# Values stationary in half-columns for two heads at once in three attentions, and a recurrence without filler products

## The chip, the cores and the metric

The kernel runs on one core of a Trainium2 chip. The metric is the device time of one execution in microseconds: median 3224.0 us of three runs (3223.61 to 3229.15).

## What is computed

Two transformer blocks of two layers each, at 512 latent tokens (and 256 context tokens in the second block), width 1024, in float32. Their large matrix products (projections, gated sums, MLPs of width 4096) take most of the time. The change touches three of the four attentions and one recurrence:

```python
# dsa: 8 heads of 64, one k and v for all heads, causal, keys chosen by an index score, ALiBi
# mla: 16 heads, q and k of 64 + 32 (rotary), v of 64, causal
# sw (gqa_attend / banded_window_attention): 8 heads of 64, 2 kv heads, a window of 3 blocks
#   of 128 keys and 256 context keys, with a sink logit in the softmax
probs = jax.nn.softmax(logits, axis=-1)
o = einsum(probs, v)
# mlstm_dir: a recurrence over chunks of 128 tokens, 4 heads of 128, in two directions
s = einsum(qc, kc) * exp(d_log - m_t)
num = inter_w * einsum(qc, c_mat) + einsum(s, vc)
h = num / max(abs(den), exp(-m_t))
c_new = carry_w * c_mat + einsum(w, kc, vc)
```

The attention of the last layer (cat, heads of 128) keeps its form.

## The kernel before

The program is written engine by engine; each engine has its own instruction list, and semaphores order them. The large products use split float32: an operand is x_hi (rounded, made by ScalarE) and x_lo (the rest, made by VectorE), and three products are summed (lines 785 to 787). Weights come by DMA into wbuf; ScalarE makes w_hi of one unit of a stage, VectorE w_lo (line 2011), and a unit of products waits for both. A stage's products are set off by `split_pair`, which takes the activations tile by tile (k) as x_lo is ready (line 2017).

The attentions dsa, mla and sw run through `attention_ahead` on TensorE and VectorE and through `attention` on ScalarE. A unit is one head of one block of 128 queries. mla and dsa go through the query blocks backwards, so key blocks per unit are 4, 3, 2, 1 (16 units each in mla, 8 each in dsa); sw has 8 units each of 4, 5, 5, 4, 2, 2. In one step of TensorE's list:

- `logits` (line 911) of unit u into psA;
- `turn_probs` of an earlier unit: its probabilities, one 128 x 128 transpose per key block (line 756), into psB. The lead is 2 units in dsa and mla, 1 in sw;
- `weigh_values` (line 928) of the unit before that: per key block one product with the transposed probabilities as the stationary 128 x 128 operand and v (128 x 64) as the streaming one, into psO, which holds two rows of ROW_H = 8 units.

VectorE masks the logits and takes their negated maximum (line 1990 in one instruction, in mla lines 1995 and 1997), ScalarE takes the exponential with its sum and copies the transposed probabilities out of psB. After a row of 8 units VectorE's `finish` takes the reciprocal of the sums (line 1976) and multiplies (line 1981) into a token-major tile. At the end of each attention TensorE turns these tiles feature-major (16 transposes in dsa, 32 in mla, 24 in sw), ScalarE copies them out, and only then are the operands of the output projection split. In mla ScalarE does that, and the first two w_hi, between the copies. dsa ends in `meet`, a barrier of all engines. In sw, TensorE first turns the recurrence's result hs, and VectorE multiplies it out (line 2584).

In the recurrence there are twelve steps (six chunks, two directions). In a step TensorE does `lstm_scores` of the step after next (first a filler product `keep_clock` of 512 columns, line 747, then four products with 4 rows, line 1225, and four scores, line 1228), `lstm_values` (lines 1249, 1250) and `lstm_keys` (line 1236). VectorE does the mask (line 2538), `lstm_finish` (lines 2516 to 2529), the state (line 2553) and two weighings (lines 2544, 2546). Four such filler calls stand ahead of or behind the stages as well.

The only place where products go to groups of columns of the array is `mod_rows` (line 1085): four products of 32 stationary columns and 384 streaming ones, each to its own 32 partitions of psO.

## Time and profile before

| what | value |
|---|---|
| median of three runs | 3224.0 us |
| the profiled execution, its own time | 3223.06 us |
| its span (first to last instruction) | 3221.2 us |
| PE busy | 3064.1 us (95%) |
| DVE busy | 1627.2 us (51%) |
| ACT busy | 1239.2 us (38%) |
| mean granted clock of TensorE | 0.972 of full speed |
| dsa, from the first logits to the first output product | 144.3 to 223.0 us |
| mla, the same | 843.4 to 949.2 us |
| recurrence, first product to last filler | 1712.7 to 1801.1 us |
| sw, first logits to first output product | 1801.1 to 1936.6 us |

The profile is one execution. PE is TensorE's products, PEld its weight loads, DVE VectorE, ACT ScalarE, POOL GpSimd. Products overlap, and their ends are modelled, so distances between starts say more than durations. PEclk is the granted clock as a share of 2.4 GHz; 0.50 is 1.2 GHz. "DVEq" or "issue" in a chain is an engine's own queue.

### The profile page before, as it was taken

The page shows a single profiled execution, that of the slowest core. Times are in us where ns is not written, and L with a number is a line of the kernel's source. Part 1 is how long each engine was busy: PE and PEld are TensorE (multiplying, and loading weights), DVE is VectorE, ACT ScalarE, POOL GpSimd, SP SyncE. Part 2 cuts the span into 40 slices and gives each one's busy share as a digit, 9 for nine tenths or more (in the row PEclk, how much of TensorE's full clock was granted, in tenths as well). Part 3 has the DMA queues.
Part 4 walks back from the last instruction along what each step waited for, and adds up shares of the span by engine and source line. Part 5 has one row for each costly group of instructions (what it writes and reads, how often), then busy time and mean ns, then how long its engine had stood idle before and what let it go on. Part 6 is the DMA issues. An engine that isn't in the chain of part 4 may idle for free.

```text
span 3221.2 us, 39495 instructions
## 1 busy us (share of the span) xinstructions
PE 3064.1 (95%) x15144; PEld 2473.4 (77%) x15144; DVE 1627.2 (51%) x2430; ACT 1239.2 (38%) x2054; POOL 155.2 (5%) x142
## 2 busy tenths in 40 slices
PE   7989999999999999999998988999999899899999
PEld 5667778867777778867886777888888776778887
DVE  4864677674454677675226443432333634344344
ACT  3444333335564333345123452432222444443333
POOL 2200000011000000010003002000000100000000
PEclk9979999999999999999998999999999999999999
DMA  5102443433202443421120001112121110022222
GB/s 195 53 19 74 163 176 137 162 108 59 73 18 75 163 176 138 161 86 53 53 79 1 1 1 53 53 54 76 52 78 52 52 55 24 1 84 99 104 84 73
DMA packets 159713, 259.22 MB, mean 80 GB/s; under 512 B 54316, under 2 KB 74154, under 8 KB 159468
## 3 DMA queue, kind: packets, MB, share of 16 engines
q1 hardware_dynamic: 157844, 252.66, 22.6%
q10 hardware_dynamic: 1628, 4.78, 0.4%
q8 instruction: 73, 1.20, 0.2%
q14 instruction: 40, 0.33, 0.0%
q0 software_dynamic: 128, 0.26, 0.0%
HBM read 255.59 MB, written 2.10 MB: 80 GB/s over the span
## 4 chain that ended last, share of the span: by engine, by line
PE 86%; DVE 6%; ACT 4%; issue 2%; DVEq 1%; ACTq 1%; POOLq 0%; DMA 0%; PEldq 0%; PEld 0%
PE psA L785 23%; PE psA L786 22%; PE psA L787 22%; PE psB L756 3%; PE psA L742 3%; PE psA L911 3%; ACT work L1316 2%; PE psO L928 2%; PE psO L873 1%; PE psA L991 1%; ACT w_hi L1316 1%; PE psA L801 1%; DVE work L2129 1%; PE psA L803 1%; PE psA L802 1%
## 5 line engine op out<-in xcount | busy, mean ns | idle before, releaser
L1316 ACT ACTIVATE w_hi<-wbuf 128x1024 fp32r<-128x1024 f32 (+1 forms) x349 | 368.2, 1057 | 1170.7 <-PE psA L787 1147.4
L785 PE MATMUL psA<-act_hi,w_hi 128*128 128x512 f32 (+1 forms) x1872 | 708.9, 379 | 44.0 <-DVE act_lo L2017 29.3
L2011 DVE TENSOR_TENSOR w_lo<-wbuf,w_hi 128x1024 fp32r<-128x1024 f32 (+1 forms) x349 | 429.3, 1233 | 567.6 <-ACT w_hi L1316 563.3
L786 PE MATMUL psA<-act_lo,w_hi 128*128 128x512 f32 (+1 forms) x1872 | 700.0, 374 | 0.0
L787 PE MATMUL psA<-act_hi,w_lo 128*128 128x512 f32 (+1 forms) x1872 | 698.6, 373 | 0.0
L785 PE MATMUL psA<-hid_hi,w_hi 128*128 128x512 f32 (+1 forms) x1280 | 477.5, 373 | 5.4 <-DVE work L2129 4.5
L786 PE MATMUL psA<-hid_lo,w_hi 128*128 128x512 f32 (+1 forms) x1280 | 472.1, 369 | 0.0
L787 PE MATMUL psA<-hid_hi,w_lo 128*128 128x512 f32 (+1 forms) x1280 | 471.5, 368 | 0.0
L785 PEld LDWEIGHTS psA<-act_hi,w_hi 128*128 128x128 f32 x1872 | 357.4, 191 | 115.0 <-issue 33.2
L786 PEld LDWEIGHTS psA<-act_lo,w_hi 128*128 128x128 f32 x1872 | 357.6, 191 | 62.6 <-issue 2.6
L787 PEld LDWEIGHTS psA<-act_hi,w_lo 128*128 128x128 f32 x1872 | 357.0, 191 | 62.2
L2129 DVE TENSOR_TENSOR work<-work,psA 128x512 f32<-128x512 f32 (+1 forms) x256 | 192.7, 753 | 262.2 <-PE psA L787 254.4
L785 PEld LDWEIGHTS psA<-hid_hi,w_hi 128*128 128x128 f32 x1280 | 241.2, 188 | 68.5 <-issue 19.9
L787 PEld LDWEIGHTS psA<-hid_hi,w_lo 128*128 128x128 f32 x1280 | 241.1, 188 | 41.4
L786 PEld LDWEIGHTS psA<-hid_lo,w_hi 128*128 128x128 f32 x1280 | 241.4, 189 | 38.3
L2151 DVE SCALAR_TENSOR_TENSOR work<-work,small 128x768 f32<-128x768 f32 x224 | 221.6, 1030 | 1.5
L1316 ACT ACTIVATE work<-psA 128x512 f32<-128x512 f32 (+2 forms) x239 | 150.5, 633 | 162.2 <-PE psA L787 145.3
L1316 ACT ACTIVATE work<-psA,small 128x128 f32<-128x128 f32 (+6 forms) x232 | 128.6, 573 | 206.4 <-DVE small L1990 80.1
L2125 DVE TENSOR_TENSOR hid_lo<-work,hid_hi 128x512 fp32r<-128x512 f32 (+1 forms) x128 | 97.1, 759 | 187.9 <-ACT hid_hi L1316 187.9
L756 PE MATMUL psB<-const,work 128*128 128x128 f32 x814 | 145.2, 304 | 43.9 <-ACT work L1316 14.8
L756 PEld LDWEIGHTS psB<-const,work 128*128 128x128 f32 x814 | 104.1, 154 | 98.6 <-issue 35.4
L1316 ACT ACTIVATE work<-work 128x512 f32<-128x512 f32 (+4 forms) x236 | 152.3, 651 | 26.9 <-DVEq L2531 7.4
(286 smaller groups left out, 3521.8 us busy)
## 6 DMA issues: line engine op xcount, KB each, us to landing
wbuf<-in_mlp_w_dram SPq DMA_DIRECT2D x64, 2048.0 KB, 8.3
work<-in_ada_w_dram SPq DMA_DIRECT2D x32, 1536.0 KB, 11.1
wbuf<-in_ab_w_in_dram SPq DMA_DIRECT2D x10, 1024.0 KB, 5.2
wbuf<-in_ple_w_gate_dram SPq DMA_DIRECT2D x4, 2048.0 KB, 7.8
wbuf<-in_c_w_in_dram SPq DMA_DIRECT2D x3, 2048.0 KB, 7.9
wbuf<-in_hy_w_in_dram SPq DMA_DIRECT2D x2, 2048.0 KB, 11.2
wbuf<-in_hy_w_out_dram SPq DMA_DIRECT2D x2, 2048.0 KB, 8.2
wbuf<-in_mla_w_out_dram SPq DMA_DIRECT2D x2, 2048.0 KB, 7.8
```

Of the source, the lines that this page charges most:

```text
L742: ins = pe.matmul(psA[0:m, s, a:b], l, r, start=(i == 0), stop=(i == len(pairs) - 1))
L756: ins = pe.transpose(psB[0:m, s, col:col + k], src, ident[0:k, 0:k])
L785: pe.matmul(psA[:, s, a:b], w_hi, x_hi[:, a:b], start=first, stop=False)
L786: pe.matmul(psA[:, s, a:b], w_hi, x_lo[:, a:b], start=False, stop=False)
L787: ins = pe.matmul(psA[:, s, a:b], w_lo, x_hi[:, a:b], start=False, stop=last)
L911: ins = pe.matmul(ps[:, a:b], l, r, start=(i == 0), stop=(i == len(pairs) - 1))
L928: ins = pe.matmul(psO[:, at:at + dv], s["turn"][:, u % 2, kb * P:kb * P + P], s["v"](qt, kb, h), start=(kb == 0), stop=(kb == nkb - 1))
L1316: return nc.scalar.activation(out, in_, func, **kw)
L2011: tt(split_target(wL, stage, u), unit(v, stage, u, g), split_target(wH, stage, u), ALU.subtract).then_inc(S["w_split"], 1)
L2125: tt(gL[n][:, m, :], hid[n][:, m % 2, :], gH[n][:, m, :], ALU.subtract).then_inc(S["hidden_set"], 1)
L2129: tt(acc[:, j, :], acc[:, j, :], ps[:, 0:n], ALU.add).then_inc(free, 1)
L2151: ins = stt(adas[:, x, :], adaw[:, e, r, :], c, adas[:, x, :], ALU.mult, ALU.add)
```

## The change

In dsa, mla and sw the value product is turned round: v (128 keys x 64 features) is the stationary operand and the transposed probabilities (128 keys x 128 queries) stream. The result is feature-major, 64 partitions; the even head of a pair goes to partitions 0 to 63, the odd one to 64 to 127, and the products of both alternate (`weigh_pair`, every second step). The reciprocals of the sums lie along queries, that is along partitions, so a new step `spread_inverse` multiplies each column of `rinv`, spread to 64 columns, with the identity; that gives them along the streaming axis, below the row's result in psO. VectorE's part is in two: `invert` (reciprocal) and `finish` (a copy of the spread inverses, 128 x 256, then a product of the same size, straight into the operand of the output projection). A row is now 4 units. The transposes and copies behind the attentions are gone, the buffers of transposed probabilities are four in place of two, and the splits of the output projections read the results where `finish` put them. In mla the mask is a table ("stair"), added by the same instruction that takes the maximum, and the first two weight units of the output projection are split during the last twelve units (`out_weights`, `out_rests`). In sw, ScalarE splits hs as before, then two weight units, then waits for the last row. In the recurrence the filler in `lstm_scores` is gone, and two small operations of `lstm_finish` become one. All other stages keep their instructions.

```diff
-ROW_H = 8
...
+ROW_H = 4
...
-                        masks=lambda qt, h: [(qt * P, qt * P + P, diag)], penalty=None,
-                        v=lambda qt, kb, h: vM[:, kb, h * MLA_V:h * MLA_V + MLA_V], prob=prob1, turn=turn1, onat=lambda qt: on1[:, qt, :],
-                        sink=False),
+                        masks=lambda qt, h: [], penalty=lambda qt: C["stair"][:, (LT - 1 - qt) * P:LAT],
+                        v=lambda qt, kb, h: vM[:, kb, h * MLA_V:h * MLA_V + MLA_V], prob=prob1, turn=lambda u: turn1[u % 4],
+                        mix=lambda qt, j: mixT1[:, j:j + 2, qt * P:qt * P + P], sink=False),
...
-                def weigh_values(u, qt, h, b0):
+                def weigh_pair(u):
+                    row, i = u // ROW_H, u % ROW_H // 2
+                    qt, b1 = us[u][1], us[u + 1][3]
                     for g in range(len(turned_groups(name, qt))):
-                        turned(pe, name, b0 + g)
-                    row = u // ROW_H
-                    if u % ROW_H == 0 and n_o[name] + row >= 2:
+                        turned(pe, name, us[u][3] + g)
+                        turned(pe, name, b1 + g)
+                    if i == 0 and n_o[name] + row >= 2:
                         pe.wait_ge(o_free, n_o[name] + row - 1)
-                    at, dv, nkb = 512 * (row % 2) + u % ROW_H * s["dv"], s["dv"], s["nkb"](qt)
+                    at, nkb = 512 * (row % 2) + P * i, s["nkb"](qt)
                     for kb in range(nkb):
-                        ins = pe.matmul(psO[:, at:at + dv], s["turn"][:, u % 2, kb * P:kb * P + P],
-                                        s["v"](qt, kb, h), start=(kb == 0), stop=(kb == nkb - 1))
-                    if u % ROW_H == ROW_H - 1:
-                        ins.then_inc(o_ready, 1)
+                        for e in range(2):
+                            pe.matmul(psO[64 * e:64 * e + 64, at:at + P], s["v"](qt, kb, us[u + e][2]),
+                                      s["turn"](u + e)[:, kb * P:kb * P + P], start=(kb == 0), stop=(kb == nkb - 1))
+
+                def spread_inverse(row):
+                    pe.wait_ge(S["rinv_set"], n_o[name] + row + 1)
+                    _, qt, h0, _ = us[ROW_H * row]
+                    at, c0 = 512 * (row % 2) + 2 * P, qt * s["H"] + h0
+                    for i in range(2):
+                        for e in range(2):
+                            c = c0 + 2 * i + e
+                            ins = pe.matmul(psO[64 * e:64 * e + 64, at + P * i:at + P * i + P],
+                                            rinv[:, c:c + 1].to_broadcast([P, 64]), ident, start=True, stop=True)
+                    ins.then_inc(o_ready, 1)
 
...
                     if step >= lead + 1:
-                        weigh_values(*us[step - lead - 1])
+                        u = step - lead - 1
+                        if u % 2 == 1:
+                            weigh_pair(u - 1)
+                        if u % ROW_H == ROW_H - 1:
+                            spread_inverse(u // ROW_H)
...
-                pe.wait_ge(S["onat_set"], n_o[name] + len(us) // ROW_H)
-                width = s["H"] * s["dv"] // P
-                if name == "sw":
-                    for t in range(width):
-                        turn("sw_o", t, [(qt * P, s["onat"](LT + qt)[:, t * P:t * P + P]) for qt in range(CT)])
-                for t in range(width):
-                    turn(name + "_o", t + (width if name == "sw" else 0),
-                         [(qt * P, s["onat"](qt)[:, t * P:t * P + P]) for qt in range(LT)])
+                pe.wait_ge(o_free, n_o[name] + len(us) // ROW_H)
...
-                keep_clock(psA[:, s, 0:512], 1)
...
-            attention("mla", lambda t: mixT1[:, t, :], out="mla_out", ahead=True)
+
+            def out_weights(u):
+                if u in (OUT_AT, OUT_AT + 2):
+                    w_hi("mla_out", (u - OUT_AT) // 2)
+
+            attention("mla", out_weights, ahead=True)
+            for k in range(KD):
+                act.wait_ge(S["onat_set"], n_o["mla"] + (LT - 1) * MLA_H // ROW_H + k // 2 + 1)
+                f(sH[LAT][:, k, :], mixT1[:, k, :], ACT.Copy).then_inc(S["act_hi"], 1)
...
-                def finish(row):
+                def invert(row):
 
                     _, qt, h0, _ = us[ROW_H * row]
-                    n, c0, dv = n_o[name] + row, qt * s["H"] + h0, s["dv"]
-                    v.wait_ge(o_ready, n + 1)
+                    c0 = qt * s["H"] + h0
+                    _, _, free, k = logit_slot(name, ROW_H * row + ROW_H - 1)
+                    v.wait_ge(free, k + 1)
                     if s["sink"]:
                         v.wait_ge(S["sink_set"], row + 1)
                         tt(rsum[:, c0:c0 + ROW_H], rsum[:, c0:c0 + ROW_H], sarg[:, c0:c0 + ROW_H], ALU.add)
                         v.drain()
-                    nc.vector.reciprocal(rinv[:, c0:c0 + ROW_H], rsum[:, c0:c0 + ROW_H])
+                    nc.vector.reciprocal(rinv[:, c0:c0 + ROW_H], rsum[:, c0:c0 + ROW_H]).then_inc(S["rinv_set"], 1)
+
+                def finish(row):
+
+                    _, qt, h0, _ = us[ROW_H * row]
+                    v.wait_ge(o_ready, n_o[name] + row + 1)
+                    at = 512 * (row % 2)
+                    total, spread = (psO[:, a:a + 2 * P].rearrange("p (i q) -> p i q", q=P) for a in (at, at + 2 * P))
+                    mixed = s["mix"](qt, h0 // 2)
+                    nc.vector.tensor_copy(mixed, spread)
                     v.drain()
-                    at = 512 * (row % 2)
-                    out, total = (x.rearrange("p (h c) -> p h c", c=dv) for x in (
-                        s["onat"](qt)[:, h0 * dv:(h0 + ROW_H) * dv], psO[:, at:at + ROW_H * dv]))
-                    tt(out, total, rinv[:, c0:c0 + ROW_H].unsqueeze(2).to_broadcast([P, ROW_H, dv]),
-                       ALU.mult).then_inc(o_free, 1)
+                    tt(mixed, total, mixed, ALU.mult).then_inc(o_free, 1)
                     v.drain().then_inc(S["onat_set"], 1)
 
                 for u, qt, h, _ in us:
...
-                    if s["sink"] and h == B_H - 1:
+                    if s["sink"] and u % ROW_H == ROW_H - 1:
                         v.drain()
-                        tt(sarg[:, c - h:c + 1], sink, nmax[:, c - h:c + 1], ALU.add).then_inc(S["sink_arg"], 1)
-                    if u % ROW_H == 3 and u > ROW_H:
-                        finish(u // ROW_H - 1)
+                        tt(sarg[:, c - ROW_H + 1:c + 1], sink[:, h - ROW_H + 1:h + 1], nmax[:, c - ROW_H + 1:c + 1],
+                           ALU.add).then_inc(S["sink_arg"], 1)
+                    if u % ROW_H == 1 and u > ROW_H:
+                        invert(u // ROW_H - 1)
+                    if u % ROW_H == 0 and u >= 2 * ROW_H:
+                        finish(u // ROW_H - 2)
                     if beside:
                         beside(qt, h, u)
+                invert(len(us) // ROW_H - 1)
+                finish(len(us) // ROW_H - 2)
                 finish(len(us) // ROW_H - 1)
...
+            def out_rests(qt, h, u):
+                if u in (OUT_AT + 1, OUT_AT + 3):
+                    w_lo("mla_out", (u - OUT_AT) // 2)
+
+            attention_ahead("mla", out_rests)
+            residual("mla_out", mixT1, 2)
             layer_norm(2, xT, "ln1_g", 8, acc, "mlp1", ahead=[("ple_g1", 0), ("ple_g1", 1)])
...
-                ts(dens, total, -1.0, None, ALU.mult)
+                floor = gcol[:, 1, 6 * dr + t, :].rearrange("p (e i) -> p e i", e=2)
+                stt(dens, total, -1.0, floor, ALU.mult, ALU.max)
                 v.drain()
                 tt(dens, dens, total, ALU.max)
-                v.drain()
```

## Rows read from the trace of the kernel before

**Rows 1.** Windows: us; busy us (count) of PE, PEld, DVE, ACT, POOL; PEclk, DMA share, GB/s.

```profile
161.00:184.00 23.00, 19.80 (x109) 15.14 (x107) 20.03 (x68) 14.90 (x34) 0.00 (x0) 0.84 0.00 0
...
204.00:213.30 9.30, 9.02 (x40) 8.25 (x39) 3.30 (x18) 5.39 (x25) 0.00 (x0) 0.50 0.00 0
...
922.00:937.60 15.60, 13.46 (x97) 11.66 (x96) 10.75 (x37) 11.09 (x53) 0.00 (x0) 1.00 0.01 2
937.60:949.20 11.60, 8.20 (x34) 5.94 (x33) 6.51 (x10) 8.83 (x15) 0.00 (x0) 0.50 0.00 1
...
1889.70:1916.00 26.30, 25.37 (x150) 18.38 (x150) 10.98 (x40) 15.09 (x55) 0.00 (x0) 1.00 0.00 1
```

**Rows 2.** Chain in a unit of mla, four key blocks: start, us, what.

```profile
866.94 0.91 PE psA L911 x2
867.85 0.44 PE psB L756 x4
868.29 0.84 PE psO L928 x8
```

**Rows 3.** Chain around the column groups of mod_rows, in mlp0.

```profile
381.76 0.23 PE psA L787
381.99 0.78 PE psO L1085 x8
382.77 0.43 PE psA L785
```

**Rows 4.** Time line of PE in sw, five key blocks: start, us, engine, line, operation.

```profile
1838.82 1.35 PE L911 MATMUL psA<-work 64*128 64x384 f32 x6
1840.11 0.76 PE L756 MATMUL psB<-const,work 128*128 128x128 f32 x5
...
1841.86 1.35 PE L911 MATMUL psA<-work 64*128 64x384 f32 x6
```

**Rows 5.** Time line of ACT in the same units of sw.

```profile
1841.20 0.79 ACT L1316 ACTIVATE work<-psA,small 128x640 f32<-128x640 f32 x1 [1.50 <-DVE small L1990]
...
1841.98 0.75 ACT L1316 ACTIVATE work<-psB 128x512 f32<-128x512 f32 x2
```

**Rows 6.** Groups by line: DVE, all of the span; busy us, mean ns, idle before.

```profile
L1976 DVE RECIPROCAL small<-small 128x8 f32<-128x8 f32 x18 | 3.6, 198 | 4.4 <-PE psO L928 3.9
...
L1981 DVE TENSOR_TENSOR work<-psO,small 128x512 f32<-128x512 f32 x14 | 9.7, 692 | 1.0
...
L2402 DVE COPY vb_ctx<-psA 128x256 f32<-128x256 f32 x1 | 0.4, 414 | 0.0
```

**Rows 7.** Time lines of the tails: dsa, mla, then sw.

```profile
218.77 2.00 ACT L1316 ACTIVATE w_hi<-wbuf 128x1024 fp32r<-128x1024 f32 x2 [0.19 <-ACTq L338]
...
936.66 0.96 PE L928 MATMUL psO<-work 128*128 128x64 f32 x4
...
949.17 0.78 PE L785 MATMUL psA<-act_hi,w_hi 128*128 128x512 f32 x1
...
945.45 3.14 DVE L2017 TENSOR_TENSOR act_lo<-work,act_hi 128x512 fp32r<-128x512 f32 x5
...
1922.64 1.14 DVE L2584 SCALAR_TENSOR_TENSOR work<-psB,vecT,work 128x512 f32<-128x512 f32 x2 [0.88 <-PE psB L756]
...
1934.19 2.35 DVE L2011 TENSOR_TENSOR w_lo<-wbuf,w_hi 128x1024 fp32r<-128x1024 f32 x2
```

**Rows 8.** Time line of PE, then of DVE, in the recurrence.

```profile
1712.72 2.07 PE L747 MATMUL psA<-const 128*128 128x512 f32 x2 [3.39 <-DVEq L338]
...
1772.30 1.02 PE L747 MATMUL psA<-const 128*128 128x512 f32 x2
...
1778.01 1.02 PE L747 MATMUL psA<-const 128*128 128x512 f32 x2
...
1777.39 0.69 DVE L2538 TENSOR_TENSOR work<-psA,const 128x512 f32<-128x512 f32 x1 [0.27 <-PE psO L1250]
...
1778.47 0.16 DVE L2520 TENSOR_TENSOR small<-small 128x4 f32<-128x4 f32 x1
```

More of the change, by code:

```diff
@@ L549, in swa_v @@
             return vb[:, t, kv * B_D:kv * B_D + B_D]
-        diag = C["before"]
         ATT = {
@@ L1580, in decay @@
                     f(t2[:, c, :], t2[:, c, :], ACT.Exp, scale=0.5).then_inc(S["sqrt_set"], 1)
-            attention("dsa", lambda t: mixT0[:, RC + t, :], decay, ahead=True)
+            attention("dsa", decay, ahead=True)
             meet(act)
@@ L1770, in _ @@
             meet(act)
-            attention("sw", lambda n: mixT2[:, 4 + n, LAT:TOK] if n < 4 else mixT2[:, n, 0:LAT], ahead=True)
-            act.drain()
+            attention("sw", ahead=True)
             for k in range(KD):
@@ L1812, in _ @@
             meet(act)
-            attention("cat", lambda t: mixT3[:, t, :], out="c_out")
+            attention("cat")
+            for n in range(C_H):
+                ps, free = get_b(act, "cat_o", n)
+                f(mixT3[:, n, :], ps, ACT.Copy).then_inc(free, 1)
+                act.drain()
+                f(sH[LAT][:, n, :], mixT3[:, n, :], ACT.Copy).then_inc(S["act_hi"], 1)
+                if n < 2:
+                    w_hi("c_out", n)
             split_linear("c_out", square_of("c_out", LAT), start=2)
@@ L2077, in add @@
                     stt(xT[:, m, 0:LAT], xT[:, m, 0:LAT], ALPHA, ps[:, 0:LAT], ALU.mult, ALU.add).then_inc(free, 1)
-                split_linear(stage, add, before=lambda: [x_lo(stage, k, mix, sH[LAT], sL[LAT]) for k in range(KD)])
+                split_linear(stage, add, before=lambda: [x_lo(stage, k, mix, sH[LAT], sL[LAT]) for k in range(KD)], start=start)
             def gated(stage, layer, n, mix=None):
```

80 lines of the change are left out of this document (34 added, 46 removed).

## The prediction

> **What bounds the kernel now.** First the busy shares and the clock of the stages [rows 1], then the chain and the time line inside one unit of each attention. TensorE is busy almost all of the time, so an attention unit is as long as its products, unless a row of [rows 1] says otherwise. 
>
> **Value products.** New form: v is stationary (64 columns), 128 query columns stream, and two heads go to the two column halves. Passes per pair of heads and key block: four before and four after. Before 4 x 0.105 = 0.42. After, one after another, 4 x 0.11 = 0.44: no gain. If the halves run at once, 0.22. The trace has one place with column groups: eight passes of 384 columns in four groups of 32 [rows 3]. Serially they would take 8 x 0.33 = 2.6 us. On the chain they take 0.78, and the ordinary product behind them 0.43 where the one before takes 0.23: 0.98 in all with its excess of 0.20. So the groups ran at once, in two rounds of 0.33. I take 0.22 per block. (The Trainium skill, page "TensorE: Matmul & The Clock Gate", section "Measured speedup vs the span model", gives three column tiles 2.38 times; here four give 2.6/0.98 = 2.6 times with the loss below, so the trace agrees.)
>
> **The price of a switch.** 0.98 - 0.66 = 0.32 us are lost for going into the column groups and out again: 0.16 a switch. A second row says the same. In sw the logits use 64 rows of the array, the other products all of it. By passes a unit with five blocks is 10 x 0.11 + 5 x 0.11 + 10 x 0.105 = 2.70 us; it takes 3.04 (1838.82 to 1841.86) [rows 4]: 0.34 for two switches. In mla, which does not switch, the same sum leaves 0.03. (The Trainium skill, page "TensorEngine Tiling (Array Packing)", section "Key Properties", says that changing the tiling mode drains TensorE; this speaks against the change and the rows agree. By its "up to 2x" for 64 columns without a drain, the result would be the cheap case under the rivals.) So mla and dsa pay 0.32 more per pair of units, sw 0.16. The rows bound it from 0 (loads prefetched over the switch) to 0.32 a switch (all of the loss on one side).
>
> **Spread of the inverse.** Per row of four units four products of 128 columns in two halves: 2 x 2 x 0.11 = 0.44 us, 0.22 per pair, with no switch of its own; serial it would be 0.88. It waits for `invert` on VectorE, which comes two units later there. In mla TensorE reaches it about 1.5 us after that; in sw, with one unit of lead, about 0.4 after.
>
> **mla.** Change per pair with n blocks: -0.42n + 0.22n + 0.32 + 0.22 = 0.54 - 0.20n. For n = 4, 3, 2: -0.26, -0.06, +0.14, eight pairs each: -1.5 us. For n = 1, TensorE is not the bound. VectorE loses one of two operations per unit (mask and maximum become one of 0.3 us), but gets two finishes of 1.0 us (copy 0.41, a product of the same size, two drains of 0.08) for one of 1.05 and the two w_lo of 1.2, and ScalarE the two w_hi of 1.0. I take -1.0 for the sixteen units (bounds -3, +2). Tail: before, 11.55 us from the last value product (936.66 + 0.96) to the first output product (949.17) [rows 7]: finish, 32 transposes, copies, two weight splits. After: spread 0.5, finish 1.0, one x_lo 0.6 (3.14/5) [rows 7], semaphores 0.3, together 2.4. Gain 9.1. The act_lo tiles then come at 0.6 us against 1.4 us of products per k, so the start holds. The clock is at 1.2 GHz in that tail now (mean 0.50) [rows 1]; after a short gap some of the slow products go: -0.5. mla: -12.1.
>
> **sw.** With five blocks, per pair: -1.00 (values) + 0.16 + 0.22 = -0.62. But the steps are now uneven, and the step without values leaves ScalarE less time. From the end of the logits (1840.11) [rows 4], the exponentials are ready after 1.9 us (ScalarE from 1841.20 for 0.79) [rows 5]. The next transposes come after 0.55 + 1.28 = 1.83, and the values need the copy behind that exponential (0.75) [rows 5], while the transposes hide only 0.55. I charge 0.3 per pair. That leaves -0.32 x 8 = -2.6. With four blocks: -0.42 + 0.3 = -0.12, x 8 = -1.0; with two, where VectorE and ScalarE already set half of the units (26.3 us for 16 units), 0. Main part -3.6, bounds 0 and -8. Tail: the 24 transposes, eight copies and the eight act_hi behind them go or start earlier. Now the second w_lo ends at 1936.54 and products start there [rows 7]. After: the finish ends 0.2 us later than now, the eight hs products of VectorE follow to 1924 (they end at 1923.8 now) [rows 7], then four x_lo of 0.87 and two w_lo of 1.15: 1929.8. Gain 6.7. sw: -10.3.
>
> **dsa.** VectorE is the bound to 204 us. In it five finishes (1.0) and five inverts (0.27) replace two finishes of 1.05 [rows 6]: +4.3. TensorE behind it runs at 1.2 GHz with 1.06 us a unit [rows 1]; switch and spread there are partly waits now, so I add nothing up to +2. Tail: from the last value product to the w_hi at 218.77 [rows 7] now 5.5 us; after it spread 1.0 (slow clock), finish 1.0, barrier 0.3: 2.4. Gain 3.1. dsa: +1.2, from -2 to +6.
>
> **Recurrence.** A step lasts 5.71 us (1772.30 to 1778.01) and TensorE has no gap in it. Without its filler of two 512-column passes (8 x 0.11) TensorE needs 4.85. VectorE takes over: it is idle 0.27 before its mask, and one small operation goes (0.16, 0.235 with its drain) [rows 8]. So the step becomes 5.71 - 0.27 - 0.235 = 5.20, and nine steps give -4.6, not -7.7. The first two fillers run at 1.2 GHz (about 1.9 each; the first, 2.07 long to its modelled end, is shown) on TensorE's path: -3.8; the third 0.9; three last finishes 0.7. Sum -10.0. If the clock rises later than now, relative to the work, up to 3 come back. The filler behind the last step stays.
>
> **Sum.** 1.2 - 12.1 - 10.0 - 10.3 = -31.2. The profiled execution took 3223.06 us (span 3221.2, 1.9 around it), 0.9 under the median of the runs, so 3191.9, and 3192.8 against the median. I say 3192.
>
> **Rivals.**
> 1. Cheap switches: the drains of [rows 3, 4] vanish behind waits and prefetched loads. 32 mla pairs x 0.32 + 24 sw pairs x 0.16 = 14 us more: 3178. Against it: two independent rows. 0.12.
> 2. Loads in the way: a pass of 128 columns is only 0.11 us long, against 0.33 in [rows 3], and each needs a new load of 64 columns. If about 0.05 per pass and half shows, a block is 0.32: 0.10 x 168 blocks (80 mla, 88 sw) = 17, so 3209. For it: in the present form the loads are the bound. Against it: half as many columns. 0.14.
> 3. Slower, halves serial: two heads' products do not overlap because each head's two passes must follow one another and the queue is kept in order. Blocks then cost 0.44 and spreads 0.88: 0.22 x 168 + 0.44 x 28 = +49, so 3241. It decides from 0.41 us per block. Against it: [rows 3] has the same two passes per group. 0.06.
> 4. Slower, clock: the attentions keep their length but TensorE does less in it. In dsa the clock fell once TensorE idled behind VectorE and did not return for 40 us although TensorE was then busy all the time. If it fell at mla's second quarter, 45 us of TensorE-bound work would last 0.8 times longer: +36, about 3228. Against it: the two-block units of sw keep 1.00 [rows 1] with waits in them, and the recurrence would be 93% busy. 0.08.
> 5. The filler did its job: the recurrence falls to 1.2 GHz now and then, each time for some 4 us of work: 3200 with three falls. Inside the main case's range. 0.06.
>
> **Chances.** Main case 0.54. A measurement of this kernel tells 0.2% (6.4 us) from no change. Faster 0.82, same 0.06, slower 0.12. The range takes in rivals 1, 2 and 5 and the bounds of dsa and sw: 3174 to 3215. Rivals 3 and 4 are left out.
>
> **What would show it.** Value products of mla with starts that let a block of two heads pass in 0.22 us, and a unit pair of n = 4 at 4.1 us against 4.38; gaps of 0.16 at each switch; the mla tail at 2.4 us; steps of 5.2 us with a waiting TensorE; granted clock 1.00 in mla, sw and the recurrence. Wrong would be: blocks over 0.3 us, mla above its present 94 us before the tail, a clock of 0.5 ahead of mla's last quarter, or a dsa stage more than 6 us longer.

## The result, and the profile after

The changed kernel takes 3193.9 us (median of 4 runs, 3187.3 to 3196.8), the kernel before 3223.8 us (median of 4, 3222.7 to 3229.2). The ratio is 0.990, with a 95% interval of 0.988 to 0.992: faster by 1.0%. Forecast were 3192 us and faster. The profiled execution took 3196.6 us, its span is 3194.8 us, so 26.4 us less than the 3221.2 us of before. One of the six runs of the full-width kernel below took 5003.1 us at a granted clock of 0.564 and is left out of its median.

The first reading cuts both spans at the same instructions of TensorE: the first product that uses an attention's output, the first logits, the first product of the recurrence (the filler in the kernel before, the scores in the changed one). The difference of each stretch stands beside the term that was forecast for it.

| stretch | before | after | change | forecast |
|---|---|---|---|---|
| start to dsa's first output product | 223.0 | 224.7 | +1.6 | +1.2 |
| to mla's first logits | 620.3 | 619.8 | -0.5 | none |
| to mla's first output product | 105.8 | 94.3 | -11.5 | -12.1 |
| to the recurrence's first product | 763.6 | 762.8 | -0.8 | none |
| to sw's first logits | 88.4 | 80.7 | -7.7 | -10.0 |
| to sw's first output product | 135.5 | 127.9 | -7.6 | -10.3 |
| to the end | 1284.6 | 1284.7 | +0.1 | none |

The windows of after that answer to [rows 1] come first (us; busy us and count of PE, PEld, DVE, ACT, POOL; PEclk, DMA share, GB/s): two of dsa, mla's last quarter and its tail, the start and the end of the recurrence, and the two-block units of sw.

```profile
161.00:184.00 23.00, 16.23 (x105) 10.10 (x106) 19.95 (x68) 14.24 (x33) 0.00 (x0) 0.86 0.00 1
204.00:216.00 12.00, 11.17 (x63) 8.26 (x59) 6.30 (x26) 5.29 (x25) 0.00 (x0) 0.50 0.01 1
920.00:935.20 15.20, 13.04 (x118) 9.42 (x116) 9.79 (x44) 11.49 (x51) 0.00 (x0) 1.00 0.01 2
935.20:938.80 3.60, 1.21 (x14) 0.83 (x14) 2.58 (x7) 3.35 (x8) 0.00 (x0) 0.97 0.01 2
1701.50:1718.20 16.70, 16.39 (x75) 15.20 (x76) 5.89 (x13) 4.59 (x16) 9.30 (x16) 0.54 0.01 1
1768.00:1774.00 6.00, 3.86 (x19) 3.59 (x18) 1.74 (x8) 1.62 (x11) 0.00 (x0) 0.50 0.00 0
1869.40:1896.80 27.40, 24.47 (x182) 13.91 (x182) 13.56 (x54) 14.38 (x53) 0.00 (x0) 1.00 0.00 1
```

dsa is as it was: VectorE busy 19.95 of 23 us, the clock at 0.86 and then 0.50, and TensorE with less to do (16.23 us in place of 19.80). mla's tail, 11.6 us at half clock before, is gone but for 3.6 us at 0.97. In the recurrence the clock is at 0.54 for the first 16.7 us and at 0.50 for seven near its end (1768.0 to 1774.9 us). The kernel before had that last fall too, but for 3.4 us alone, here in its own window:

```profile
1791.00:1794.40 3.40, 3.40 (x16) 2.90 (x14) 0.45 (x3) 0.56 (x4) 0.00 (x0) 0.50 0.00 0
```

The chain in mla with four key blocks (start, us, what) answers to [rows 2]:

```profile
853.22 0.86 PE psA L911 x2
854.08 0.44 PE psB L761 x4
854.52 1.02 PE psO L931 x16
855.54 0.43 PE psO L941 x8
```

Sixteen value passes, four blocks of two heads, take 1.02 us, where two heads took 1.68. The spread of the inverses takes 0.43. It comes once in four units, so a pair of units is 4.04 us long on the mean, by the distance of the spreads (8.07 us per four units), against 4.38.

The time line of the tails answers to [rows 7]: first mla (its last value product, the last finish on VectorE, the low parts of the input, the first output product), then sw (spread, finish, the last two of the eight hs products, low parts, first output product).

```profile
935.93 0.44 PE L931 MATMUL psO<-work 128*64 128x128 f32 x4 [0.46 <-ACT work L1324]
...
936.85 0.42 DVE L1998 COPY work<-psO 128x256 f32<-128x256 f32 x1 [0.73 <-PE psO L941]
937.35 0.42 DVE L2000 TENSOR_TENSOR work<-psO,work 128x256 f32<-128x256 f32 x1
937.91 2.50 DVE L2040 TENSOR_TENSOR act_lo<-work,act_hi 128x512 fp32r<-128x512 f32 x4
...
938.75 0.77 PE L790 MATMUL psA<-act_hi,w_hi 128*128 128x512 f32 x1 [1.94 <-DVE act_lo L2040]
...
1896.27 0.64 PE L941 MATMUL psO<-const,small 128*64 128x128 f32 x8
...
1897.45 0.42 DVE L2000 TENSOR_TENSOR work<-psO,work 128x256 f32<-128x256 f32 x1
...
1903.16 1.14 DVE L2611 SCALAR_TENSOR_TENSOR work<-psB,vecT,work 128x512 f32<-128x512 f32 x2 [0.88 <-PE psB L761]
...
1904.22 3.55 DVE L2040 TENSOR_TENSOR act_lo<-work,act_hi 128x768 fp32r<-128x768 f32 x4
...
1907.69 2.35 DVE L2034 TENSOR_TENSOR w_lo<-wbuf,w_hi 128x1024 fp32r<-128x1024 f32 x2
...
1910.14 0.77 PE L790 MATMUL psA<-act_hi,w_hi 128*128 128x512 f32 x1 [6.60 <-DVE w_lo L2034]
```

mla: from the end of the last value product (936.37) to 938.75 are 2.4 us, before 11.55. The finish is a copy of 0.42 and a product of 0.42. sw: from the last value product, where the spread begins (1896.27), to 1910.14 are 13.9 us, before 20.6.

The time lines of ACT and PE in sw with five key blocks answer to [rows 4, 5]:

```profile
1809.07 0.79 ACT L1324 ACTIVATE pT<-psA,small 128x640 f32<-128x640 f32 x1 [2.08 <-DVE small L2008]
...
1809.85 0.76 ACT L1324 ACTIVATE work<-psB 128x512 f32<-128x512 f32 x2
...
1810.58 0.74 PE L761 MATMUL psB<-const,pT 128*128 128x128 f32 x5 [0.56 <-ACT work L1324]
```

TensorE has a wait here that before had not: 0.56 us for ScalarE's copy. A pair of units is 6.02 us long on the mean of those with and without a spread, against 6.08 before (twice the 3.04 of [rows 4]). TensorE's waits in the changed kernel's sw are these (who waits, for whom; us in total, times, longest), first in the units of five blocks (1802 to 1849 us), then in those of two (1870 to 1896.8 us):

```profile
PE psB L761 <- ACT work L1324: 3.9, 7, 0.6
```

```profile
PE psB L761 <- ACT pT L1324: 1.7, 7, 0.2
PE psO L931 <- ACT work L1324: 0.6, 1, 0.6
PE psO L941 <- DVE small L1989: 0.5, 3, 0.2
```

The first eight units, of four blocks, have none (1782 to 1802 us), and those of the second four-block stretch one of 0.5 us.

The masks of the recurrence's step on VectorE stand closer together; the first two rows are of after, the last two of the kernel before, 5.71 us apart:

```profile
1759.06 0.68 DVE L2565 TENSOR_TENSOR work<-psA,const 128x512 f32<-128x512 f32 x1
...
1764.17 0.68 DVE L2565 TENSOR_TENSOR work<-psA,const 128x512 f32<-128x512 f32 x1
...
1765.96 0.69 DVE L2538 TENSOR_TENSOR work<-psA,const 128x512 f32<-128x512 f32 x1 [0.26 <-PE psO L1250]
...
1771.67 0.69 DVE L2538 TENSOR_TENSOR work<-psA,const 128x512 f32<-128x512 f32 x1 [0.26 <-PE psO L1250]
```

A step is 5.11 us long, and VectorE no longer waits for TensorE ahead of its mask.

### The profile page after: what moved, and what is told of

Same layout as the page of the kernel before. It is cut to its first block, busy times and chain, and to the rows that moved or that the text cites. A ratio compares the mean times of both kernels' runs of the same rounds, so it can differ in the third digit from the quotient of the medians.

```text
span 3194.8 us, 39955 instructions
## 1 busy us (share of the span) xinstructions
PE 3025.9 (95%) x15336; PEld 2420.6 (76%) x15336; DVE 1626.7 (51%) x2502; ACT 1223.6 (38%) x2040; POOL 154.3 (5%) x142
## 4 chain that ended last, share of the span: by engine, by line
PE 83%; DVE 7%; ACT 4%; issue 2%; DVEq 2%; ACTq 0%; POOLq 0%; DMA 0%; PEldq 0%; PEld 0%
PE psA L790 23%; PE psA L791 22%; PE psA L792 22%; PE psA L747 3%; PE psB L761 2%; ACT work L1324 2%; PE psA L911 2%; PE psO L931 1%; PE psO L878 1%; PE psA L1000 1%; DVE psA L2008 1%; ACT w_hi L1324 1%; PE psA L806 1%; DVE work L2152 1%; PE psA L808 1%
## 5 line engine op out<-in xcount | busy, mean ns | idle before, releaser
L1324 ACT ACTIVATE work<-psA 128x512 f32<-128x512 f32 (+2 forms) x239 | 150.3, 632 | 162.8 <-PE psA L792 145.3
L790 PE MATMUL psA<-ab_hi,ab_w_hi 128*128 128x512 f32 (+1 forms) x384 | 131.2, 342 | 6.3 <-DVE ab_lo L2040 6.2
L791 PE MATMUL psA<-ab_lo,ab_w_hi 128*128 128x512 f32 (+1 forms) x384 | 131.0, 341 | 0.0
L792 PE MATMUL psA<-ab_hi,ab_w_lo 128*128 128x512 f32 (+1 forms) x384 | 130.4, 340 | 0.0
```

Source lines behind the costliest of these rows:

```text
L790: pe.matmul(psA[:, s, a:b], w_hi, x_hi[:, a:b], start=first, stop=False)
L791: pe.matmul(psA[:, s, a:b], w_hi, x_lo[:, a:b], start=False, stop=False)
L792: ins = pe.matmul(psA[:, s, a:b], w_lo, x_hi[:, a:b], start=False, stop=last)
L1324: return nc.scalar.activation(out, in_, func, **kw)
```

## Experiments

Times are the median of 4 to 10 runs; the kernel before gave 3223.7 to 3224.5 us beside each. The lengths of stretches are cut as in the table above, each in the one execution that was profiled.

**How much is the filler, and how much the shorter denominator?** One kernel puts the filler back, one takes it out of the kernel before.

```
 def lstm_scores(u, j, dr, t):
     ...
     pe.wait_ge(a_free[s], c)
+    keep_clock(psA[:, s, 0:512], 1)
```

> The changed kernel with one edit undone: the filler product stands again ahead of the scores in each of the twelve steps of the recurrence; the attentions stay as changed. By the theory that the filler lay on TensorE's path in every step, the stretch from the recurrence's first product to sw's first logits goes back from 80.7 us to that of the kernel before, 88.4 us: +7.7 us, so about 3202 us; 5.4 of it in the nine steady steps (a step of 5.7 in place of 5.1 us), the rest ahead of the first. By the rival that the shorter mask and denominator on VectorE brought the gain, it stays near 81 us.

> The kernel before with the filler product taken out of the recurrence's steps and nothing else changed. The theory expects most of 7.7 us, about 3217 us: the steps fall from 5.7 to some 5.2 us, a little over the changed kernel's 5.1, because the two small operations in VectorE's step stay. The rival expects the steps to stay at 5.7 us, and the time at 3224 us, or above it if the clock falls without the filler.

Measured with the filler back: 3203.1 us (ratio 0.994, 0.992 to 0.995), recurrence 86.4 us, steps of 5.71 us. Without it in the kernel before: 3219.2 us (0.998, 0.997 to 0.999), recurrence 83.1 us. The masks of that run, again on VectorE:

```profile
1763.20 0.68 DVE L2537 TENSOR_TENSOR work<-psA,const 128x512 f32<-128x512 f32 x1
...
1768.55 0.68 DVE L2537 TENSOR_TENSOR work<-psA,const 128x512 f32<-128x512 f32 x1
```

The step is 5.35 us, and the wait for TensorE ahead of the mask is gone. So the filler alone was worth 0.36 us a step, and the shorter denominator the other 0.24. The rival is right only once TensorE no longer sets the step: with the filler back, the shorter denominator gives nothing in the steps. The expected return to 88.4 us came only to 86.4. Of the missing 2 us, 1.5 are in the start (17.5 us from the first filler to the third mask, 19.0 in the kernel before) and 0.5 at the end; the next experiment says why the start differs.

**Is the recurrence short of its forecast by the clock?** Fillers only where TensorE is idle:

```
 def head_norms(stage, first, n, tile, sq, mean, rot):
     ...
         for m in range(p + 2, min(p + 4, n)):
             norm(m)
+        if stage == "ab_n" and p == 0:
+            keep_clock(psO[:, 0:512], 2)
         for m in (p, p + 1):
+            if stage == "ab_n" and m == 4:
+                keep_clock(psO[:, 0:512], 2)
             ...
+        if stage == "ab_n":
+            keep_clock(psO[:, 0:512], 2 if p == 0 else 0 if p == 2 else 4)
 ...
 for step in lstm_steps:
     ...
+    if u >= LSTM_KV:
+        pe.wait_ge(S["state_set"], LSTM_KV + 1)
+        keep_clock(psB[:, 1, :], 3 if u == LSTM_KV else 2)
     lstm_values(*step)
```

> The changed kernel with filler products only where TensorE is idle around the recurrence: two to four of 0.88 us in each of the idle stretches of the head norms ahead of it (1678 to 1701 us), and three and two ahead of the values of the last two steps; none in the steps themselves. The theory that the recurrence is short of its forecast by the clock (0.50 for the first 15 us, and from 1768 to 1775 us) expects the clock at 1.00 through both: the start falls from 16.6 to some 11 us and the end from 10.9 to some 9, so about 7 us less, 3187 us. The rival that the start hangs on ScalarE and GpSimd expects under 2 us.

Measured: 3189.1 us (0.990, 0.988 to 0.991), recurrence 73.5 us. The windows of its start and its end, with the columns of the windows above:

```profile
1699.00:1710.70 11.70, 11.00 (x75) 10.22 (x76) 5.98 (x12) 4.60 (x16) 8.82 (x16) 0.85 0.01 2
1759.00:1765.00 6.00, 5.15 (x32) 3.90 (x33) 3.09 (x10) 3.18 (x19) 0.00 (x0) 1.00 0.00 0
```

From the first scores to the third mask it is 11.7 us in place of 16.6, from the last mask to sw's first logits 15.8 in place of 18.0. Expected was a clock of 1.00 through both; in the start it still stood at 0.50 for 3.4 us. The clock was the cause, and the nine kernels of this study that run the changed recurrence as it is say the same without a filler. In three of them the clock rose 10 us after the first scores, and the third mask came after 14.2 us. In two it rose after 15.3 us (mask after 16.6), and in four after about 18 (mask after 17.7). They took 77.6 to 83.0 us for the recurrence; 73.5 lies below all of them. So against another execution than the changed kernel's own, 7.1 us could have been 4 or 9. Over the long stretch from mla's first output product to sw's first logits the filled kernel took 838.0 us and those nine 837.6 to 849.6, so there it is only as good as the best of them.

**Why does sw gain so little?** First theory: the copy waits behind the exponential. In ScalarE's part of the attention:

```
 for u, qt, h, b0 in us:
     ...
+    if name == "sw" and u >= 1:
+        evacuate(*us[u - 1])
     act.wait_ge(S[name + "_max"], u + 1)
     ...
-    if u >= 1:
+    if u >= 1 and name != "sw":
         evacuate(*us[u - 1])
```

> The changed kernel with ScalarE in sw copying the turned blocks of the unit before ahead of the exponential of this one, not behind it. The theory that a unit of five blocks waits 0.56 us for this copy, because it needs both banks of psB, expects this wait to go: sw from first logits to first output product 128 us to 122 to 124 us, about 3190 us. The rival: the exponential now stands behind the copy, the turns of the next unit behind the exponential, and the pair gets no shorter than 6.0 us or longer (sw up to 135 us, about 3201 us).

Measured: 3194.4 us (0.991, 0.990 to 0.993), sw 127.9 us as before the edit. Neither theory is whole. By the starts of the transposes, sixteen units of five blocks shrank by 2.3 us and the units of four blocks on both sides grew by the same: in the first eight of them TensorE now waited 0.30 us for the exponential in every second step. The wait moved, so its cause isn't the order on ScalarE. The second experiment spreads the values over both steps of a pair (part 1 of `weigh_pair` is the first two or three blocks, part 2 the rest):

```
 if step >= lead + 1:
     u = step - lead - 1
+    if name == "sw" and u % 2 == 0 and u >= 2:
+        weigh_pair(u - 2, 2)
+        if u % ROW_H == 0:
+            spread_inverse(u // ROW_H - 1)
     if u % 2 == 1:
-        weigh_pair(u - 1)
+        weigh_pair(u - 1, 1 if name == "sw" and u < len(us) - 1 else None)
```

> The changed kernel with sw's value products of a pair of four or five blocks spread over two steps (three blocks, or two, behind the second unit's turning; the rest, and the spread of the inverses, behind the next unit's). It tells the two causes of sw's 0.56 us wait apart. If it is that all values of a pair stand in every second step, so that the step between is 2.0 us long on TensorE and ScalarE, with some 1.9 us of work behind VectorE's mask for each unit, can't keep it, the wait goes: -0.56 us and +0.23 to +0.32 for the one more change of column mode, -0.25 to -0.33 us for each of 20 pairs, sw's stretch 127.9 to some 122 us. If it is that a unit of five blocks takes both banks of psB whatever stands between, the wait stays and the change of mode is added: some 133 us.

Measured: sw 122.4 us, 5.5 less; 3193.3 us in all (0.991, 0.989 to 0.993). By the starts of the transposes 3.5 us of it lie in the units of five blocks, none in those of four, and 1.7 in those of two, where the edit moves nothing but the spread of the inverses to the next step. The last 0.5 is in the tail and isn't the edit's: six kernels with the changed sw untouched took 127.5 us too. The chain of a pair in the kernel that has this edit with others (the last of this section):

```profile
1818.84 0.70 PE psB L761 x5
1819.53 0.81 PE psO L932 x12
1820.34 1.28 PE psA L911 x6
1821.62 0.70 PE psB L761 x5
1822.32 0.59 PE psO L932 x8
1822.91 1.28 PE psA L911 x6
1824.19 0.71 PE psB L761 x5
```

All of it is TensorE, and the pair (one without a spread) is 5.35 us from transposes to transposes. So with five blocks the cause is the bunching: logits and transposes alone make a step of 2.0 us, too short for mask, exponential and copies behind it, and with the values the other step is over 3 us, in which those engines idle. A second condition stands beside it and was not tried by itself: the transposes of five blocks fill both banks of psB and wait for the copy that empties them, those of four fill one. With four blocks the step without values is even shorter (1.8 us), and TensorE waits but once. In the units of two blocks only the spread moved, so their 1.7 us are its share. That the median fell by only 0.5 us for 5.5 in sw is the spread of other stretches (last section).

**Do the halves overlap, and on what does it hang?** One kernel sends both heads to one half, one puts them one after another.

```
 for kb in range(nkb):
     for e in range(2):
-        pe.matmul(psO[64 * e:64 * e + 64, at:at + P], ...,
-                  start=(kb == 0), stop=(kb == nkb - 1))
+        pe.matmul(psO[0:64, at:at + P], ...,
+                  start=(kb == 0 and e == 0), stop=(kb == nkb - 1 and e == 1))
```

> The changed kernel with the value products of both heads of a pair sent to the same half of the output's columns, summed there (so the second half of the mixed heads isn't computed). If the two halves work at once, as read from 1.02 us for sixteen products, each block now costs 0.43 us in place of 0.22: +0.22 us for each of mla's 80 and sw's 88 pairs of blocks, +37 us less what waits in sw absorb, some 3222 to 3232 us; mla's stretch goes from 94 to 112 us. If the halves never overlapped, the time stays at 3194 us.

```
-for kb in range(nkb):
-    for e in range(2):
+for e in range(2):
+    for kb in range(nkb):
```

> The changed kernel with the products of a pair ordered head by head, all blocks of the first head and then all of the second, in place of alternating. If TensorE overlaps only a product with the next one in its queue, only the one meeting of the two heads overlaps, and the time goes up almost as if there were one half: +28 to +37 us. The rival, that each half has a queue of its own deep enough to let the second head start while the first has blocks left, expects 3194 us.

Measured with one half: 3227.3 us (1.001, 1.000 to 1.002), mla 110.6 us (+16.3), sw 145.3 (+17.4). Head by head: 3208.2 us (0.995, 0.993 to 0.997), mla 100.3 (+6.0), sw 137.0 (+9.1). The value products on the chain at four blocks, head by head and then in one half:

```profile
850.97 1.51 PE psO L931 x16
```

```profile
850.61 1.89 PE psO L931 x16
```

**What does a change of the column mode cost?** One kernel stays in full width in mla (the lines below hold for mla alone); two weigh four units at a time.

```
-pe.matmul(psO[64 * e:64 * e + 64, at:at + P], s["v"](qt, kb, us[u + e][2]), ...)
+pe.matmul(psO[:, at:at + P], vM[:, kb, us[u][2] * MLA_V:us[u][2] * MLA_V + P], ...)
 ...
-rinv[:, c:c + 1].to_broadcast([P, 64])
+rinv[:, c:c + 1].to_broadcast([P, 128])
```

> The changed kernel with mla's value products in all 128 columns: stationary the 128 value columns of the pair of heads, for each head's weights in turn, summed (so what they give isn't mla's), and the spread of the inverses in all columns too. TensorE then never changes its column mode in mla. No overlap: 80 pairs of blocks by +0.22 us = +17.6, sixteen spreads by +0.44 = +7.0; no change of mode: 32 pairs by -0.32 us = -10.2 if the price read from the rows is right. Sum +14.4 us: mla's stretch 94.3 to 108.7 us, about 3208 us. The rival, that changing the mode costs nothing, expects +24.6 us: 118.9 and 3219 us.

```
+u = step - lead - 1
+if name == "mla" and step >= lead + 1 and u % 4 == 3:
+    weigh_pair(u - 3)
+    weigh_pair(u - 1)
 if 0 <= step - lead < len(us):
     turn_probs(*us[step - lead])
```

> The changed kernel with mla's values weighed four units at a time, ahead of the turning of the next unit, in place of two at a time: half as many changes of column mode. By the price of 0.32 us for in and out, 16 pairs of changes fewer are -5 us: mla's stretch 94.3 to some 89 us, about 3189 us. The rival: the values now wait for ScalarE's copy of the last turned blocks, which the turning of the next unit had covered, 0.3 to 0.5 us sixteen times, and the time stays where it is.

The second form adds `spread_inverse(u // ROW_H)` behind the two pairs, ahead of `turn_probs`:

> The changed kernel with mla's values weighed four units at a time and the spread of their inverses right behind them, ahead of the turning of the next unit: one stay in the half-column mode for each four units, where the changed kernel has two, and where the run before this one still had two (its spread stood behind the turning). By the price from the rows, 0.32 us for in and out, 16 stays fewer give -5 us; by that from the run in full width, 0.23 us, -3.7 us: mla's stretch 94.3 to 89.2 or 90.6 us. The rival expects the wait for ScalarE's last copy or for the inverse to take the place of the price: 94 to 95 us.

Measured in full width: 3212.7 us (median of five; 0.996, 0.995 to 0.998), mla 111.4 us, +17.1 where 14.4 was expected. Four units need 9.67 us with four blocks where the changed kernel needs 8.07: +1.60 in place of the 8 x 0.22 + 0.44 = 2.20 that the lost overlap costs. The 0.60 are two stays in the half-column mode, 0.30 each for in and out; with three blocks (7.48 against 6.35 us) 0.31, with two 0.19. On the mean of all 32 stays it is (24.6 - 17.1)/32 = 0.23, so the expected 0.32 was too much for the short units. The first kernel by four units, 3198.5 us, gained nothing (mla 94.7): the transposes stood between values and spread, so it had as many stays as before. The second has half as many: 3195.5 us (0.991, 0.990 to 0.993), mla 92.0 us. Four units take 7.68, 5.95 and 4.36 us with four, three and two blocks, against 8.07, 6.35 and 4.62: 0.39, 0.40 and 0.26 per stay. At the end of the two-block units it is 4.2 us ahead, and then it loses 2 of them in the last quarter. There its clock also stood at 0.50 for 3.4 us (926.0 to 929.4), which it did not in the changed kernel; how much of the 2 us that is was not separated. The waits of TensorE are, first in this kernel and then in the changed one (who waits, for whom; us in total, times, longest):

```profile
PE psB L761 <- ACT const L1329: 1.8, 4, 1.1
PE psO L931 <- ACT work L1329: 1.3, 2, 0.8
```

```profile
PE psB L761 <- ACT const L1324: 1.1, 2, 0.7
PE psO L931 <- ACT work L1324: 0.7, 2, 0.5
```

The rival's wait is real, but only where a unit is short.

**Do the two weight splits hide inside mla's last quarter?**

```
-attention_ahead("mla", out_rests)
-residual("mla_out", mixT1, 2)
+attention_ahead("mla")
+residual("mla_out", mixT1)
 ...
-attention("mla", out_weights, ahead=True)
+attention("mla", ahead=True)
 ...
-split_linear("mla_out", start=2)
+split_linear("mla_out")
```

> The changed kernel with the high and low parts of mla_out's first two weight tiles split behind mla's attention, as in the kernel before, and no longer inside its last quarter. If that move hides as forecast, undoing it costs the two splits on each engine behind the tail, 1.9 us on ScalarE at least and up to 3 us: mla's stretch 94.3 to 96 to 97 us, about 3197 us. If the splits inside the last quarter (0.94 us on ScalarE and 1.08 us on VectorE each) held the attention up by as much as they save, no change.

Measured: mla 97.9 us, +3.6; 3201.8 us (0.993, 0.992 to 0.995). The move pays more than expected, but the splits hide only in part: without them the last quarter is 1.7 us shorter (13.3 us between its first and last logits in place of 15.0), and the tail behind it is 5.3 us longer. In that tail ScalarE's two w_hi (1.99 us from 937.56 on) and VectorE's two w_lo (2.36 us from 938.64 on) now stand ahead of the first output product (941.75).

**All that helped, together.** Fillers in the gaps; in mla four units at a time where a unit has two blocks or more; sw's values over two steps.

> The changed kernel with what the runs point to, together: filler products in the idle stretches ahead of the recurrence and ahead of the values of its last two steps; mla's values and spread by four units at a time where a unit has two to four blocks (in the last quarter by two, since the copies were waited for there); sw's values of a pair over two steps. If the three don't meet: mla's stretch 94.3 to 90.1 us (4.2 gained up to the last quarter), the recurrence with the stretch ahead of it 843.5 to 838 us, sw's 127.9 to 122.3 us, in all -15.4 us: about 3178 us. If what is gained in mla is lost to ScalarE in its last quarter as before, -13 us: 3181 us.

Measured: 3179.7 us (median of 4, 3177.6 to 3183.1), ratio 0.987 (0.985 to 0.988): 14 us under the changed kernel, 44 under the one before. mla 90.2 us, recurrence 73.5, sw 122.8. The gains add up; in the profiled executions it is 18.6 us under the changed kernel, of which 4.1 are mla, 7.1 the recurrence and 5.1 sw; the rest lies in stretches that no edit touched.

## Why the prediction was right, and where it was not

**Right in sum.** 3192 forecast, 3193.9 measured; against the profiled execution, by which the sum was made, 3191.9 and 3196.6. The four terms fell short by 0.4 (dsa), 0.6 (mla), 2.3 (recurrence) and 2.7 us (sw), and stretches without a term gave 1.2 back. That the medians lie within 2 us is partly luck: the same changed kernel took 3187.3 to 3196.8 us, and inside mla and sw larger misses cancel.

**Value products: right.** 0.22 us per block of two heads was forecast and is shown twice, by 0.87 us more for four pairs of blocks in one half and by the length of the stretches. Rivals 2 (loads in the way) and 3 (halves serial) fall. Rival 3 had a point: the overlap does hang on the queue's order, and 15 us of it are lost if the heads aren't alternated.

**The switch: right.** 0.32 us for in and out was forecast; 0.30 and 0.39 were measured with four blocks. Rival 1 (switches for nothing) falls: it would have made the full-width kernel 24.6 us slower in mla, and it was 17.1. With two blocks per unit the price is less, 0.19 to 0.26. The Trainium skill, page "TensorEngine Tiling (Array Packing)", section "Key Properties", says that a change of the tiling mode drains TensorE; that a stay costs 0.19 to 0.40 us here agrees with it.

**mla: right in sum, the main part by luck.** The main part fell by 2.4 us (forecast 2.5), the tail by 9.2 (forecast 9.1, and 0.5 for the clock). But by the starts of the logits the first three quarters gave 4.3 us in place of 1.5, since a pair of four blocks fell by 0.34 us and not by 0.26 (with three blocks by 0.12 and not by 0.06). And the last quarter, which was to give 1.0, took 2.0 more; 1.7 of that are the two weight splits in it. The move of the splits is worth 3.6 us all the same, 5.3 in the tail less 1.7.

**Recurrence: the step was right, the clock was not.** Nine steps were to fall from 5.71 to 5.20 us and fell to 5.11: the filler gave 0.36 us in place of 0.27, the denominator 0.24 as forecast 0.235. The mis-sized term is the start, -3.8 and -0.9 for its three fillers, of which 2.3 came (18.96 us to the third mask before, 16.64 after): the clock stayed at 0.50 up to 1716.8 us, 15.3 us after the first scores, where before it rose 11.4 us after them. The prediction had named this ("up to 3 come back"). It had not named the end, where 0.7 was to be gained and nothing was (17.98 us from the last mask to sw's first logits before, 18.04 after), since the fall there lasts 6.9 us in place of 3.4. Where it lasted 3.4 us with the shorter denominator (the kernel with the copy first), the end took 17.5. These are the last two steps on TensorE, with the product that the fall of the clock meets between them:

```profile
1766.88 0.46 PE L1257 MATMUL psO<-const,work 128*128 128x129 f32 x2 [2.99 <-DVE work L2556]
...
1767.85 0.45 PE L1257 MATMUL psO<-const,work 128*128 128x129 f32 x2
1768.10 0.64 PE L1258 MATMUL psO<-work 128*128 128x129 f32 x2
...
1771.73 0.77 PE L1257 MATMUL psO<-pT,work 128*128 128x129 f32 x2 [2.14 <-DVE work L2556]
```

TensorE idles 2.99 and 2.14 us ahead of them (3.06 and 2.38 in the kernel before), and from 1768 us on a product takes 0.64 us in place of 0.39. Fillers in these gaps and in those ahead of the recurrence gave 7.1 us back against the changed kernel's own execution. Rival 5, falls inside the steps, did not come: no fall in the nine steps, with TensorE busy 45.45 of 46 us by its records.

**sw: the failed step.** The main part was to fall by 3.6 us and fell by 0.8; the tail is right (6.7, as forecast). By the starts of the transposes the units of four blocks gave 3.0 us (forecast 1.0), those of five 0.4 (forecast 2.6), and those of two took 2.6 more (forecast 0). The step that failed is "I charge 0.3 per pair", with the 0 for two blocks. With five blocks the wait for ScalarE is 0.56 us a pair, and that in the prediction's own sum gives what was measured: -0.62 + 0.56 = -0.06, and 6.02 us stand against 6.08. With four blocks, where 0.3 was charged as well, TensorE waits but once. With two it waits 2.8 us in all, for the exponential, a copy and the inverses, where before it had waited 0.9. The mechanism was the one named, uneven steps, and the size was off. With five blocks the prediction set ScalarE's work against the transposes that follow, but the copy that TensorE waits for is that of the unit before, which stands behind the exponential; both must fit into a step of 2.0 us. It didn't name that only five blocks need both banks of psB, and it charged four blocks too. Putting the copy first moved the wait, and evening the steps out took it away.

**dsa: right, with luck,** +1.6 against +1.2, with VectorE as the bound. Ten kernels of this study run the changed dsa, and from the first logits to the first output product three of them took 77.3 us and seven, the changed one among them, 80.2 (before: 78.9); in the three the clock was at 1.00 for some 7 us from about 210 us on. In one of the three the same term would have come out as a gain. Rival 4, a fall of the clock in mla, did not come: 1.00 up to the tail.

## What to carry to other kernels

Two heads with 64 value columns can share TensorE at half the cost per block (0.22 us in place of 0.44), if their products alternate; batch them so that the mode is entered seldom, since every stay costs 0.2 to 0.4 us, which is as much as one or two blocks save. But batching bunches the work: where other engines follow each unit in lockstep, spread the batch over the steps, even at the price of one more change of mode. And when a filler is taken out, keep it where TensorE still idles: there no cost showed (764.5 us from mla's first output product to the first scores, where the nine kernels without it took 759.9 to 766.6), and in the steps it cost 0.36 us each.

## What the runs showed of the hardware that was not expected

**The halves look ahead by about two blocks.** Order the products head by head and 0.37 to 0.44 us of them still overlap, whatever the number of blocks (1.51 us for sixteen passes against 1.02 and 1.89).

**The same instructions get the clock at different moments.** Nine kernels of this study, the changed one among them, run the same instructions from mla's first output product to sw's first logits, and took 837.6 to 849.6 us for it. In the recurrence's start the granted clock rose some 10 us after the first scores in one and some 18 us in another, though in both the last product ahead of them starts 4.3 us before them. Two windows of the kernel with the copy first (first scores at 1700.5 us), then the same windows of the first one by four units (1701.6 us):

```profile
1710.00:1715.00 5.00, 4.74 (x40) 4.37 (x39) 3.13 (x8) 1.59 (x6) 2.84 (x4) 0.95 0.01 2
1715.00:1720.00 5.00, 5.00 (x43) 4.76 (x43) 4.44 (x15) 2.29 (x8) 2.34 (x4) 1.00 0.00 0
```

```profile
1710.00:1715.00 5.00, 4.74 (x21) 4.22 (x21) 3.95 (x9) 2.30 (x8) 2.85 (x4) 0.50 0.01 2
1715.00:1720.00 5.00, 5.00 (x28) 4.98 (x27) 0.70 (x2) 0.00 (x0) 0.00 (x0) 0.57 0.00 0
```

The first has its matmuls at 0.95 of the clock while the second is still at 0.50. Other stretches scatter too: from sw's first output product to the end all fourteen kernels run the same instructions and took 1283.0 to 1287.3 us. This is why a gain in one stretch shows in the median only in part, and why the readings here rest on stretches. Of sw's 5.5 us, 3.3 are left in the profiled span, since the stretch behind sw took 1287.3 us there and 1284.6 in the changed kernel's. What sets the moment was not tried and stays open.
